# Modulation blocks 6 to 9 of the first layer as split products on TensorE instead of multiply-adds on VectorE, with the mixer's order rewritten around them

## The reference

```python
def adaln(cvec, w, b):
    m = jax.nn.silu(cvec) @ w + b
    return tuple(jnp.split(m[:, None, :], N_MOD, axis=-1))
...
    sh1, sc1, g1, sh2, sc2, g2 = adaln(c, ada_w[layer], ada_b[layer])
    ...
        hx = modulate(x, sh1, sc1)
        mx = ab_mixer(hx, *ab)
    x = x + g1 * mx
    hx2 = modulate(x, sh2, sc2)
    ...
def ab_mixer(h, w_in, v_gain, w_s, b_s, w_pool, p_scale, w_out):
    z = h @ w_in
    ya = chunk_gmlp(jax.nn.gelu(z[..., :2 * A_WIDTH], approximate=False), v_gain, w_s, b_s)
    yb = multiscale_pool(z[..., 2 * A_WIDTH:], w_pool, p_scale)
    return jnp.concatenate([ya, yb], axis=-1) @ w_out
```

## Time and profile before

| | |
|---|---|
| median of 3 runs | 1773.2 us (1771.94 to 1785.75) |
| the profiled execution | 1776.53 us |
| its span | 1774.7 us |
| mean granted clock of TensorE in it | 0.952 of full |

### The profile page before, as it was taken

One profiled execution on the slowest core, in us unless ns is written; L12 is line 12 of the kernel. 1 busy time (PEld: TensorE's weight loads), 2 busy tenths in 40 slices (PEclk: granted clock), 3 DMA queues, 4 the chain that ended last, 5 costly groups with the idle time before them and its releaser, 6 DMA issues.

```text
span 1774.7 us, 21478 instructions
## 1 busy us (share of the span) xinstructions
PE 1601.0 (90%) x8461; PEld 1323.5 (75%) x8462; DVE 1321.5 (74%) x1449; ACT 843.4 (48%) x826; POOL 0.2 (0%) x4
## 2 busy tenths in 40 slices
PE   4988989999999977799779999999999998998994
PEld 1876777788888767566667888787887786886883
DVE  5867657777777854766458798888888888878886
ACT  5431242211112153422356777676767666666663
POOL 0000000000000000000000000000000000000000
PEclk9988999999999978889889999999999999999998
DMA  9534335344646431000098999999989898998992
GB/s 350 197 134 135 126 100 185 119 144 166 213 166 213 134 98 48 1 1 1 19 320 305 337 352 346 309 354 337 339 315 334 314 329 312 327 307 302 345 318 80
DMA packets 209452, 391.80 MB, mean 221 GB/s; under 512 B 7818, under 2 KB 82220, under 8 KB 209348
## 3 DMA queue, kind: packets, MB, share of 16 engines
q1 hardware_dynamic: 204826, 385.77, 62.9%
q10 hardware_dynamic: 4522, 4.61, 0.8%
HBM read 389.30 MB, written 1.05 MB: 220 GB/s over the span
## 4 chain that ended last, share of the span: by engine, by line
PE 78%; DVE 12%; ACT 5%; issue 3%; DMA 1%; SPq 1%; DVEq 0%; ACTq 0%
PE bank L573 20%; PE bank L575 19%; PE bank L574 19%; DVE lo L532 5%; ACT hi L526 3%; PE bank L2129 3%; PE bank L2130 3%; PE bank L1995 2%; PE bank L1984 2%; PE bank L2151 1%; PE bank L2169 1%; DVE X L1644 1%; PE bank L2170 1%; PE bank L1770 1%; PE bank L2001 1%
## 5 line engine op out<-in xcount | busy, mean ns | idle before, releaser
L532 DVE TENSOR_TENSOR lo<-raw,hi 128x2048 fp32r<-128x2048 f32 x328 | 742.4, 2280 | 210.7 <-ACT hi L526 210.0
L526 ACT ACTIVATE hi<-raw 128x2048 fp32r<-128x2048 f32 x328 | 624.4, 1908 | 488.9 <-PE bank L575 415.5
L2129 PE MATMUL bank<-hi,xg 128*128 128x512 f32 (+1 forms) x384 | 144.4, 383 | 15.6 <-DVE lo L532 15.5
L1185 DVE SCALAR_TENSOR_TENSOR acc<-raw,cs,acc 128x512 f32<-128x512 f32 x216 | 146.6, 746 | 1.4
L573 PE MATMUL bank<-Hhi,hi 128*128 128x512 f32 x352 | 140.8, 400 | 2.8 <-issue 2.8
L2130 PE MATMUL bank<-lo,xg 128*128 128x512 f32 (+1 forms) x384 | 141.5, 376 | 0.0
L575 PE MATMUL bank<-Hhi,lo 128*128 128x512 f32 x352 | 139.0, 395 | 0.0
L574 PE MATMUL bank<-Hlo,hi 128*128 128x512 f32 x352 | 138.1, 392 | 0.0
L573 PE MATMUL bank<-H3h,hi 128*128 128x256 f32 x352 | 100.2, 285 | 19.9 <-DVE lo L532 19.7
L573 PE MATMUL bank<-hi,xg 128*128 128x512 f32 (+1 forms) x288 | 109.9, 382 | 3.3 <-DVE X L1644 2.3
L574 PE MATMUL bank<-lo,xg 128*128 128x512 f32 (+1 forms) x288 | 108.7, 378 | 0.0
(11 more groups left out here) (366 smaller groups left out, 3047.5 us busy)
## 6 DMA issues: line engine op xcount, KB each, us to landing
raw<-in_moe_w_gate_dram SPq DMA_DIRECT2D x88, 1024.0 KB, 5.9
raw<-in_moe_w_up_dram SPq DMA_DIRECT2D x88, 1024.0 KB, 6.5
raw<-in_moe_w_down_dram SPq DMA_DIRECT2D x88, 1024.0 KB, 6.6
raw<-in_ada_w_dram SPq DMA_DIRECT2D x48, 1024.0 KB, 5.7
raw<-in_ffn_w_gate_dram SPq DMA_DIRECT2D x11, 1024.0 KB, 5.4
raw<-in_ffn_w_up_dram SPq DMA_DIRECT2D x11, 1024.0 KB, 5.5
raw<-in_ffn_w_down_dram SPq DMA_DIRECT2D x11, 1024.0 KB, 5.0
raw<-in_ab_w_in_dram SPq DMA_DIRECT2D x6, 1024.0 KB, 8.7
```

The costliest lines, as they stand in the source:

```text
L526: nc.scalar.activation(hi[n0 % SPL][:, 0:size], raw[slot][:, 0:size], ACT.Copy).then_inc(hi_ready, 1)
L532: nc.vector.tensor_tensor(lo[n0 % SPL][:, 0:size], raw[slot][:, 0:size], hi[n0 % SPL][:, 0:size].bitcast(F32), ALU.subtract).then_inc(lo_r ...
L1185: ins = V.scalar_tensor_tensor(out=sum_, in0=w_, scalar=c_, in1=biased[:, place_, :] if h == 0 and i < 2 else sum_, op0=ALU.mult, op1=ALU.add)
L2129: T.matmul(b[:, 0:n_], xg[:, kk, 0:P], wh[:, k, :], start=(kk == 0), stop=False, skip_group_check=True)
```

## The change

Blocks 6 to 9 take the form of blocks 0 to 3: their slabs are split by ScalarE and VectorE, `rows_of`, `mod_row`, `columns_of` and `mod_col` replace `direct` and `spread`. Their bias rows come by four loads of their own. The mixer's order on each engine, the order of the slabs and that of the banks are rewritten: `gate(0, 4)` moves ahead of the gelu of slab 3; `rows_of(6)` stands behind input slab 3, `rows_of(7)` behind slab 4, `rows_of(8)` around the pooling, `rows_of(9)` ahead of the output projection; the four `pool`s stand together, then the `ya` transposes, then the four `yb`; pooling uses banks 4 to 6; the projection starts before `yb` is ready and waits for it at its second slab.

```diff
+MIX_SLABS = [("ab_in", 0), ("ada0", (4, 0)), ("ab_in", 1), ("ab_in", 2), ("ada0", (4, 1)), ("ada0", (5, 0)), ("ab_in", 3), ("ada0", (5, 1)),
+             ("ada0", (6, 0)), ("ada0", (6, 1)), ("ab_in", 4), ("ada0", (7, 0)), ("ada0", (7, 1)), ("ab_in", 5),
+             ("ada0", (8, 0)), ("ada0", (8, 1)), ("ada0", (9, 0)), ("ada0", (9, 1))] + [("ab_out", (h, q)) for h in range(2) for q in range(2)]
...
-DIRECT = [(0, cb) for cb in range(4, 10)] + [block for step in FFN_BLOCKS for block in step]
+DIRECT = [(0, cb) for cb in (4, 5)] + [block for step in FFN_BLOCKS for block in step]
...
-    return stage == "ada1" or stage == "ada0" and key[0] >= 4
+    return stage == "ada1" or stage == "ada0" and key[0] in GATE_BLOCKS
... (bank_order)
-    out.append(("ada0", 1, [(("bc", cb, who), 5 + who) for cb in (4, 5) for who in range(2)] + [(("col", cb), b) for cb, b in ((6, 7), (7, 5), (8, 6), (9, 7))]))
+    out.append(("ada0", 1, [(("bc", cb, who), 5 + who) for cb in (4, 5) for who in range(2)]))
+    for cb in (6, 7):
+        out.append(("ada0", 1, [(("m", cb), cb - 1, (cb, 1)), (("col", cb), 7)]))
...
-    for g in (0, 1, 2, 3, 4):
-        out.append(("ab_pool", 1, [(g, g)] if g < 4 else []))
-        out.append(("ab_yb", 1, [(g - 1, (3 + g) % 5)] if g >= 1 else []))
-    out.append(("ab_ya", 1, [(g, (3 + g) % 5) for g in range(4)]))
-    out.append(("ab_out", 1, [((h, t), (4 * h + t) % 5) + (((h, 1),) if t == 3 else ()) for h in range(2) for t in range(NT)]))
+    out.append(("ab_pool", 1, [(g, (4, 5, 6, 4)[g]) for g in range(4)]))
+    out.append(("ada0", 1, [(("m", 8), 7, (8, 1))]))
+    out.append(("ab_ya", 1, [(g, g) for g in range(4)]))
+    out.append(("ab_yb", 1, [(g, (5, 6, 4, 5)[g]) for g in range(4)]))
+    out.append(("ada0", 1, [(("m", 9), 6, (9, 1)), (("col", 8), 7), (("col", 9), 7)]))
+    for h in range(2):
+        out.append(("ab_out", 1, [((h, t), ((0, 1, 2, 3), (5, 6, 4, 0))[h][t]) + (((h, 1),) if t == 3 else ()) for t in range(NT)]))
... (sync)
+                    if key == (6, 0):
+                        for cb in range(2):
+                            await_emptied(sp, "ada0", ("col", cb))
+                        for cb in range(6, 10):
+                            sp.dma_start(mod_rows(cb)[4:5], a["ada_b"][0:1, 512 * cb:512 * cb + 512]).then_inc(later_bias_in, 16)
... (scalar)
+            splits("ab_in", 1, 2)
+            gelu(0)
+            splits("ab_in", 3)
+            gelu(1)
+            splits("ada0", (6, 0))
+            gelu(2)
+            splits("ada0", (6, 1))
+            gate(0, 4)
+            gelu(3)
+            splits("ab_in", 4)
... (the four squares of v, then the root)
+            gate(0, 5)
+            splits("ada0", (7, 0), (7, 1))
+            splits("ab_in", 5)
+            splits("ada0", (8, 0), (8, 1), (9, 0), (9, 1))
+            splits("ab_out", (0, 0))
+            for g in range(4):
+                nc.scalar.activation(Hhi[:, g, :], full(act, "ab_ya", g)[:], ACT.Copy).then_inc(ya_hi, 1)
... (the four yb copies)
+            splits("ab_out", (0, 1), (1, 0), (1, 1))
... (vector)
+            splits("ab_in", 1)
+            direct(0, 4, 0)
+            splits("ab_in", 2)
+            direct(0, 4, 1)
+            direct(0, 5, 0)
+            splits("ab_in", 3)
+            direct(0, 5, 1)
+            splits("ada0", (6, 0), (6, 1))
+            splits("ab_in", 4)
... (the norm of v)
+            mod_row(6)
+            splits("ada0", (7, 0), (7, 1))
+            pool_rows(4)
+            splits("ab_in", 5)
+            mod_col(0, 6)
+            mod_row(7)
+            splits("ada0", (8, 0), (8, 1))
+            pool_rows(5)
+            mod_col(0, 7)
+            splits("ada0", (9, 0))
... (the u step)
+            splits("ada0", (9, 1))
             pooled(0)
-            for g in range(4):
-                if g < 3:
-                    pooled(g + 1)
-                yb(g)
+            pooled(1)
+            splits("ab_out", (0, 0))
+            mod_row(8)
... (the four ya subtractions)
-            mod_col(0, 6)
-            mod_col(0, 7)
-            direct(0, 8, 0)
-            direct(0, 8, 1)
+            pooled(2)
+            pooled(3)
+            for g in range(4):
+                yb(g)
+            splits("ab_out", (0, 1))
+            mod_row(9)
             splits("ab_out", (1, 0), (1, 1))
...
-            residuals(0, (0, 1))
-            direct(0, 9, 0)
-            residuals(0, (2, 3))
-            direct(0, 9, 1)
+            residuals(0, range(4))
             mod_col(0, 8)
+            mod_col(0, 9)
             residuals(1, range(4))
-            mod_col(0, 9)
... (tensor)
                 if j in (2, 3):
                     spread(0, 2 + j)
+                if j in (3, 4):
+                    for h in range(2):
+                        rows_of(3 + j, h)
+                if j >= 4:
+                    columns_of(2 + j)
... (ab_s)
+            rows_of(8, 0)
+            for g in range(4):
+                pool(g)
+            rows_of(8, 1)
... (ya transposes)
-            spread(0, 6)
-            spread(0, 7)
-            pe.wait_ge(y_ready, 4)
+            for g in range(4):
+                yb(g)
+            rows_of(9, 0)
+            rows_of(9, 1)
             for g in range(4):
                 await_emptied(pe, "ab_ya", g)
             for h in range(2):
-                project("ab_out", [((h, 0), 512), ((h, 1), 512)], 4, range(4), tok(Hhi, Hlo), lambda t: (h, t))
-                spread(0, 8 + h)
+                project("ab_out", [((h, 0), 512), ((h, 1), 512)], 4, range(4), tok(Hhi, Hlo), lambda t: (h, t),
+                        late=None if h else (y_ready, 4))
+                if h == 0:
+                    columns_of(8)
+                    columns_of(9)
```

More of the change, by code:

```diff
@@ L470, in build @@
         l1_in, fgain_in, bias_in = sem("layer1_consts_in"), sem("fgain_in"), [sem(f"bias_in{i}") for i in range(2)]
-        first_bias_in = sem("first_bias_in")
+        first_bias_in, later_bias_in = sem("first_bias_in"), sem("later_bias_in")
         silu_c, c_hi, c_lo = sem("silu_c"), sem("c_hi"), sem("c_lo")
@@ L602, in mod_rows @@
         def mod_rows(cb):
+            if cb >= 8:
+                return gateM[0:5, 512 * (cb - 8):512 * (cb - 7)]
             return (zp if cb in (2, 3) else mrow)[0:5, cb % 2, :]
@@ L810, in _ @@
             norm(0, 0, 0)
[L811 to L829, removed]
@@ L830, in _, with gelu @@
-            splits("ab_out", (0, 0), (0, 1), (1, 0))
+            def gelu(j):
+                for t in range(NT):
+                    dst = (u if j < 2 else v)[:, t, (j % 2) * 256:(j % 2 + 1) * 256]
+                    emptied(nc.scalar.activation(dst, full(act, "ab_in", (j, t))[:, 0:256], ACT.Gelu), "ab_in", (j, t))
+            splits("ab_in", 1, 2)
[5 more added lines that the diff above has]
+            splits("ada0", (6, 1))
@@ new lines, in _ @@
+            gate(0, 4)
+            gelu(3)
+            splits("ab_in", 4)
+            for t in range(NT):
+                await_emptied(act, "ab_in", (3, t))
+                if t:
+                    act.wait_ge(sumsq[4], t)
+                else:
+                    await_emptied(act, "wsT", "wsT")
+                nc.scalar.activation(vsq, v[:, t, :], ACT.Square, accum_out=ssq[:, t, 1:2]).then_inc(sumsq[4], 1)
+            act.wait_ge(meansq[4], 1)
+            nc.scalar.activation(root[:, :, 1:2], rstd[:, :, 1:2], ACT.Sqrt).then_inc(rooted[4], 1)
@@ L836, in _ @@
                 emptied(nc.scalar.activation(ybtmp[:, g % 2, :], b[:], ACT.Copy, scale=bscale_col[:, g:g + 1]), "ab_yb", g)
-            for g in range(4):
-                nc.scalar.activation(Hhi[:, g, :], full(act, "ab_ya", g)[:], ACT.Copy).then_inc(ya_hi, 1)
-            splits("ab_out", (1, 1))
+            splits("ab_out", (0, 1), (1, 0), (1, 1))
             roots(1, x_ready[0])
@@ L1215, in _, with pool_rows @@
             await_emptied(dve, "wsT", "wsT")
[L1216 to L1234, removed]
+            def pool_rows(j):
+                for t in range(NT):
+                    b = full(dve, "ab_in", (j, t))
+                    emptied(V.tensor_copy(zp[:, t, (j - 4) * 256:(j - 3) * 256], b[:, 0:256]), "ab_in", (j, t))
+            splits("ab_in", 1)
[7 more added lines that the diff above has]
+            splits("ab_in", 4)
+            dve.wait_ge(sumsq[4], NT)
+            inverse_root(4, [(rstd[:, :, 1:2], ssq[:, :, 1:2], AW)])
+            chain.mark(V.reciprocal(rstd[:, :, 1:2], root[:, :, 1:2]))
+            chain.wait()
+            for t in range(NT):
+                V.scalar_tensor_tensor(out=v[:, t, :], in0=v[:, t, :], scalar=rstd[:, t, 1:2], in1=vgain[:],
+                                       op0=ALU.mult, op1=ALU.mult).then_inc(v_ready, 1)
+            mod_row(6)
[8 more added lines that the diff above has]
+            splits("ada0", (9, 0))
             for t in range(NT):
@@ L1742, in columns_of @@
                 await_emptied(pe, "ada0", ("m", cb))
```

(19 more changed lines are left out.)

6 lines of the change are left out of this document (removed).

## The result

| | before | after |
|---|---|---|
| median | 1773.2 us | 1784.5 us (1780.5 to 1799.2, 13 runs) |
| ratio, 95% interval | | 1.0069 [1.0047, 1.0090] |
| span of the profiled execution | 1774.7 us | 1797.0 us |

The change made the kernel 0.7% slower, 11 us in the median. The profiled execution after was the longest of its 13; what it has beyond the median isn't in the mixer, as the experiments' last part shows.

A forecast was written before the change was run, and what follows sets the result against it. It took TensorE's finish of the mixer's output projection as the bound: 7.7 - 1.4 - 0.7 + 1.3 = +6.9 us there, so 1776.53 becomes 1783.4, and with the median 3.3 us lower, 1780 us; range 1768 to 1789.

The forecast's parts named there:

- my own case: Whole kernel: the change makes it 3 to 11 us slower, chance 0.56.
- rival (2): Mixer, from 153 us into the projection: TensorE's clock oscillates and half speed holds, +13.6 us, so 1787; chance 0.17.
- the wait at the gate copy: Before `rows_of(6)`: TensorE still waits for `gate(0, 5)` to empty bank 5, idle 105.0 to 110.5 us, then half clock.
- the gap before slab 5: Input slabs: 2.7 us of waiting and 1.6 of slow clock are exchanged for 4.2 us of TensorE work.
- the relief of VectorE: Mixer: VectorE has some 22 us less work, and the `u` step ends 2.6 us earlier.
- the relay: From the `u` step to the projection: TensorE, ScalarE and VectorE wait on each other; projection starts at 176, +7.7 us.
- bank 6: Before `yb(1)`: only `pooled(2)` empties this bank, at 165.7 us, so TensorE idles 5.4 us.
- bank 7: Output projection: `columns_of(9)` waits for `mod_col(0, 8)`, which stands behind four residuals, +1.3 us.
- +6.9: End of the output projection: predicted delay in us, the sum 7.7 - 1.4 - 0.7 + 1.3.
- the bound for the first of these: Relay: if the clock falls at the first short gap (152.7 to 154.6 us), 5 to 7 us more.
- a sign of being wrong: Behind the mixer: the prediction is wrong if times after 240 us shift against each other.
- Rival (1): Mixer: the relay doesn't bind and gaps absorb the added work, end 3.8 us earlier, 1769; chance 0.15.

The follow-up runs named there:

- e1: Changed kernel with four pooling buffers instead of two, so VectorE copies all four pooled banks in a row: ratio 1.0007 to the kernel before, 1772.5 us.
- e2: Changed kernel with the copy of gate block 5 moved ahead of ScalarE's squares: ratio 1.0015 to the kernel before, 1776.5 us.
- e3: Changed kernel with `columns_of(8)` ahead of the projection and `mod_col(8)` right behind `mod_row(9)`: ratio 1.0037 to the kernel before, 1780.2 us.
- e4: Changed kernel with the edits of e1, e2 and e3 together: ratio 0.9965 to the kernel before, 1765.1 us.
- e6: Changed kernel with `rows_of` for blocks 6 to 9 doing one of four k-blocks: ratio 1.0010 to the kernel before, 1775.4 us.
- e8: e4 with VectorE's four pooled copies ahead of the split of half block (9, 1): ratio 0.9944 to the kernel before, 1761.8 us.
- e10: e8 with `rows_of` for blocks 6 to 9 doing one of four k-blocks: ratio 0.9939 to the kernel before, 1761.6 us.
- e9: e5 with VectorE's half block (7, 1) and output slab splits behind `u` and pooling, block 7's sum behind the projection's first half: ratio 0.9927, 1760.5 us.
- e5: Kernel before, with only the copy of gate block 4 moved ahead of the gelu of slab 3: ratio 0.9960, 1764.4 us.

## Why the prediction was right

I had 1780 us, the measured median is 1784.5, inside 1768 to 1789, and within 1% as given 0.93. The size was less good: my own case, 3 to 11 us slower, was just passed, by 11.3 us between the medians and 12.2 by the ratio, and the result lies between it and rival (2)'s 13.6. Set against the marks of its walk:

| mark | predicted | after |
|---|---|---|
| idle before `rows_of(6)` | 5.5, to 110.5 | 5.61, to 109.90 |
| slab 5's end | 143.1, no wait before it | 143.2, no wait |
| `u` step | 147.3 to 151.5 | 147.50 to 151.72 |
| wait for bank 4 | to 154.6 | 2.14, to 154.92 |
| idle before the second `yb` | 5.4, to 165.7 | 5.34, to 167.50 |
| projection starts | 176 | 178.92 |
| projection ends | 223 | 228.1 |

The mechanism of each step was right: the wait at the gate copy moved and kept its length; the gap before slab 5 was exchanged for work; the relief of VectorE gave 2.4 us at `u` and was lost in the relay; bank 6 tied `yb(1)` to `pooled(2)`; bank 7 tied `columns_of(9)` to the residuals. e1, e2 and e3 took these ties away one at a time and got 10.1, 8.0 and 3.7 us back (1.6 of the 8.0 and 1.5 of the 3.7 by the clock elsewhere).

What was mis-sized is the clock, three times, +6.9 for 12.0 us. I let it stay at full speed behind the 2.1 us gap before pool 3; it fell, and `rows_of(8, 1)` took 3.4 us instead of 1.9. I took 4.5 us for `rows_of(9)`; it took 5.7 (173.25 to 178.92). And I counted -1.4 us for the projection without a slow stretch, but it has one, in its second half, behind the pair of `columns_of`: 23.9 us (204.22 to 228.1) where 22.4 would do. Together 1.5 + 1.2 + 1.5 = 4.2 of the 5.1 missing us, within the 5 to 7 us that I had given as the bound for the first of these. Of the rest, `columns_of` was priced at 0.5 us and took 0.98 (131.10 to 132.08), 1.9 us for four, against a wait for bank 7 of 0.70 us where I had 1.3. How much of the clock's part belongs to the new order and how much to this one execution isn't shown: the same gap of 2.14 us was followed by no half clock in e2 and e4, and the same gap of 0.70 us by none in e6.

I had also called it a sign of being wrong if times after 240 us shift against each other. In SwiGLU they don't, but in attention the two profiles do, by 10.2 us. Since after's own 13 executions lie 18.6 us apart, the sign was too coarse to be read from one profile.

Rival (1), absorbed gaps, is refuted for this order and comes true in e8, where the relay doesn't bind: its mixer is 10.1 us shorter than before, against the 3.8 that I had worked out while keeping the gate's wait. Rival (2), the oscillating clock, happened in part: two more falls than I had, each over after about 3 us, not a half speed held through. The Trainium skill's rule ("TensorE: Matmul & The Clock Gate", A second HAM failure mode: psum-queue depth-cycling) is borne out in kind by this profile, where the clock fell behind gaps of 0.70 and 2.14 us among short groups; in the profiles of e2, e4 and e6 it stayed up behind gaps of the same length.

## What to carry to other kernels

Moving work off a busy engine is worth only what stands ahead of a waiting critical engine; look for that wait first, since here moving one copy of 1 us ahead of a norm, with nothing rewritten, gave 7 us of the whole time (some 8 in the mixer, and 3 more of clock that may be chance), where the rewriting of four blocks cost 12. Work that goes onto the bound engine must have a gap assigned to it, and each bank, buffer or ring place that it shares adds a wait of its own: walk the new order engine by engine before building it. And a gap of TensorE of even one or two microseconds among short products can have some 1.5 us of half clock behind it, or none: give it a range, and compare two profiles mark by mark to see which of them had it.

## What the runs showed of the hardware

That the clock can fall behind so little was new to me: 0.70 us of idle with 16 small pieces around it at 201 to 204 us, 1.5 us lost. e1 and e2 have the same gap and the same fall (at 194 and 197 us), e6 has the gap and no fall. Behind the gap of 2.14 us before pool 3 the clock fell in after and e1 and stayed up in e2 and e4; in e3 it fell as the gap ended (0.54 from 154 to 155 us). With no gap at all it fell behind 32 one-column products before and in e9, and not behind the same 32 in e5. So a gap or a group of short products doesn't settle by itself whether the clock falls; what does, no run here tests. With the seam's gap gone (e3, e4, e8, e10) it stayed at full speed there each time.

The same instructions of attention took 236.7 to 252.5 us in eleven profiled executions. A single profile's span can therefore be off by more than this whole change; its stretches can be compared one by one.
